# RWKV section of a three-block decoder: low-rank products taken from the unnormalised split, token mixes in two operations through PSUM, key scaling moved ahead

## The reference, cut to what matters

```python
hn = rms_norm(h, g[1])
xx = pad(hn, one token)[:, :-1] - hn              # previous token minus this one
xm = hn[None] + xx[None] * mix[:, None, None, :]  # six token mixes
xr, xw, xk, xv, xa, xg = xm
r, k, v = xr @ w_r, xk @ w_k, xv @ w_v            # 1024 x 1024 each
w_log = -softplus(-(w0 + tanh(xw @ w1) @ w2)) - 0.5   # 1024 -> 64 -> 1024
a = sigmoid(a0 + (xa @ a1) @ a2)                      # 1024 -> 64 -> 1024
g = sigmoid(xg @ g1) @ g2                             # 1024 -> 160 -> 1024
kk = normalised per head (k * k_k);  k = k * (1 + (a - 1) * k_a)
decay = exp(-exp(w_log))
y = scan over tokens(r, decay, k, v, -kk, kk * a);  bonus = sum(r * k * r_k) * v
```

## Time and profile before

| | us |
|---|---|
| median of 3 runs (1629.85 to 1635.62) | 1633.55 |
| the profiled execution, device time | 1638.21 |
| its span on the core | 1636.4 |
| TensorE busy in it | 1573.2 |
| POOL busy | 1132.7 |
| ACT busy | 775.7 |
| DVE busy | 659.9 |

### The profile page before, as it was taken

The page is one execution under the profiler, slowest core; times in us unless marked ns, Lnnn a source line. Parts: engine busy times, 40 slices in busy tenths (PEclk is TensorE's granted clock), DMA queues, the critical chain, the costliest instruction groups (busy, mean ns, idle before and its releaser), DMA issues.

```text
span 1636.4 us, 40796 instructions
## 1 busy us (share of the span) xinstructions
PE 1573.2 (96%) x16206; PEld 1498.9 (92%) x16206; DVE 659.9 (40%) x1534; ACT 775.7 (47%) x1271; POOL 1132.7 (69%) x835
## 2 busy tenths in 40 slices
PE   6999989899999999999999999999999999999998
PEld 6999989688887999999999987599999988799998
DVE  4332067664545433223332257743351434433200
ACT  5444447832314544445444442654445534655532
POOL 6787858683505787788777785068878984468885
PEclk9999999898999999999999999999999998999999
DMA  6453533320012554465544641055545542235552
GB/s 251 178 181 128 182 115 112 129 88 3 3 54 78 181 179 163 142 208 180 179 155 146 213 160 52 2 196 201 183 147 185 193 158 90 94 107 195 187 180 77
DMA packets 37910, 231.34 MB, mean 141 GB/s; under 512 B 4527, under 2 KB 6680, under 8 KB 16552
## 3 DMA queue, kind: packets, MB, share of 16 engines
...
...
## 4 chain that ended last, share of the span: by engine, by line
PE 90%; DVE 5%; issue 2%; POOL 2%; ACT 1%; DMA 1%; SPq 0%; DVEq 0%; POOLq 0%; ACTq 0%
PE PS L768 74%; PE PS L767 2%; POOL wlo L722 1%; PE PS L999 1%; PE PS L1006 1%; PE PS L1014 1%; PE PS L1376 1%; PE PS L1164 1%; PE PS L1155 1%; DMA raw<-w_f_in_in 1%; PE PS L783 0%; PE PS L1038 0%; PE PS L1044 0%; DVE ktmp L1983 0%; PE PS L989 0%
## 5 line engine op out<-in xcount | busy, mean ns | idle before, releaser
L722 POOL TENSOR_TENSOR wlo<-raw,whi 128x256 fp32r<-128x256 f32 (+2 forms) x759 | 1085.9, 1464 | 445.4 <-ACT whi L2524 418.2
L768 PE MATMUL PS<-xh,whi 128*128 128x272 f32 (+1 forms) x2336 | 676.2, 289 | 23.2 <-POOL wlo L722 17.9
L768 PE MATMUL PS<-xl,whi 128*128 128x272 f32 (+1 forms) x2336 | 668.4, 286 | 0.0
L768 PE MATMUL PS<-xh,wlo 128*128 128x272 f32 (+1 forms) x2336 | 667.8, 286 | 0.0
L2524 ACT ACTIVATE whi<-raw 128x1024 fp32r<-128x1024 f32 x472 | 459.7, 982 | 390.1 <-PE PS L768 363.5
L768 PEld LDWEIGHTS PS<-xh,whi 128*128 128x128 f32 x2336 | 440.4, 189 | 31.8 <-issue 24.3
L768 PEld LDWEIGHTS PS<-xh,wlo 128*128 128x128 f32 x2336 | 442.2, 189 | 0.0
L768 PEld LDWEIGHTS PS<-xl,whi 128*128 128x128 f32 x2336 | 441.6, 189 | 0.6
L768 PE MATMUL PS<-hid_h,whi 128*128 128x272 f32 (+1 forms) x960 | 273.6, 285 | 1.6 <-POOL wlo L722 1.6
L768 PE MATMUL PS<-hid_h,wlo 128*128 128x272 f32 (+1 forms) x960 | 273.8, 285 | 0.0
L768 PE MATMUL PS<-hid_l,whi 128*128 128x272 f32 (+1 forms) x960 | 272.8, 284 | 0.0
...
## 6 DMA issues: line engine op xcount, KB each, us to landing
...
```

The source lines that it names most:

```text
L722: last = nc.gpsimd.tensor_tensor(wlo[U % SPL][:, piece], raw[U % RAW][:, piece], whi[U % SPL][:, piece].bitcast(F32), ALU.subtract)
L768: mm(out, a, b, start=start and n == 0, stop=stop and n == 2, **kw)
```

## The change

- Low-rank products: `lora_wa` and `lora_g` leave the list of units. Their weights are loaded once, and during `f0_dn` (one of 8 chunks per output chunk) DVE scales them by mix and by 1 - mix into PSUM, ACT copies the high parts, DVE subtracts the low parts (`lora_weights`). `f0_dn` now also splits `h` times the gain into `xh[0]`, `xl[0]`, and its DVE and ACT loops are written out. TensorE takes the products for decay, a and gate from that split; DVE multiplies both results by `rstd` and adds the one shifted by a token (`lora_drain`).
- The order on TensorE becomes: first products of decay and a, half of the gate's, `wa2` with the gate's other half in three blocks between, `rk_k` (first unit with both output tiles for each input chunk), `rk_r`, `rk_v`. The 64 constant passes go.
- Token mixes: three in place of six. `hn` has a zero column in front, `xx` is gone, and a mix is a `tensor_scalar` of `hn` into PSUM and a `scalar_tensor_tensor` that adds `hn` of the token before. `rstd` is copied to PSUM, from where `hn` is made.
- Head sums move between units 2 and 3 of `rk_r`, `spread_kk` ahead of `rk_v`, `bonus_sums` to the middle of `rk_v`; the key's factor gets a buffer of its own (`Bk`), the keys are scaled in front of `a_g`, and the bonus products wait for `rk_r` by pairs. ACT's copy of `g2` moves behind the bonus copies.

```diff
-    ("rk_k", 4, 4, 2048), ("lora_wa", 1, 1, 1024), ("rk_r", 4, 4, 2048), ("wa2", 1, 8, 1024),
-    ("lora_g", 1, 1, 1280), ("rk_v", 4, 4, 2048),
+    ("wa2", 1, 8, 1024), ("rk_k", 4, 4, 2048), ("rk_r", 4, 4, 2048), ("rk_v", 4, 4, 2048),
...
+                if name == "f0_in" and i is None and u == 5:
+                    sp.dma_start(raw_wa[:, :, :], t["w_lora_wa"][0].rearrange("p (k c) -> p k c", k=KC)).then_inc(s_lraw, 16)
...
+            sp.dma_start(raw_g[:, :, :], t["w_lora_g"][0].rearrange("p (k c) -> p k c", k=KC)).then_inc(s_lraw, 16)
...
+                if paired and u == 0:
...
+                    for k in range(KC):
+                        pe.wait_ge(s_x, X0[x] + k + 1)
+                        for mi in range(2):
+                            c = mi * 1024 + k * 128
+                            last = products(PS[:, bank(G) + mi, 0:n], weights(U, ALLR, slice(c, c + 128)),
+                                            (xh[b][:, k, 0:n], xl[b][:, k, 0:n]), k == 0, k == KC - 1)
+                    last.then_inc(s_unit, 2)
+                    continue
...
+    def lora(w_, which, out, at, m, ks):
+        h_, l_ = w_
+        for k in ks:
+            c = k * h_.shape[2] // KC + at
+            last = products(PS[0:m, out, 0:T], (h_[:, which, c:c + m], l_[:, which, c:c + m]),
+                            (xh[0][:, k, :], xl[0][:, k, :]), k == 0, k == KC - 1)
+        return last
...
+    pe.wait_ge(s_ldr, KC)
+    first_lora(0, range(KC - 1))
     norm_sum("rk", T)
-    constants(44, PS[:, 1, 0:128])
-    project("rk_k", T, 1, "m0", wide=True)
-
-    U, G = U0["lora_wa"], G0["lora_wa"]
-    pe.wait_ge(s_lo, 2 * U + 2)
...
-    pe.wait_ge(s_free, G - 1)
-    constants(20, PS[:, bank(G), 0:128])
-    project("rk_r", T, 3, "m3")
+    first_lora(1, range(KC - 1))
+    first_lora(0, (KC - 1,))
+    first_lora(1, (KC - 1,)).then_inc(s_lora, 1)
+    gate_lora(0, range(KC)).then_inc(s_lora, 1)
...
     for m in range(KC):
+        if m in (2, 4, 6):
+            if m == 2:
+                pe.wait_ge(s_ldr, KC + 3)
+            last = gate_lora(1, {2: range(3), 4: range(3, 6), 6: range(6, 8)}[m])
+            if m == 6:
+                last.then_inc(s_lora, 1)
         G = G0["wa2"] + m
         pe.wait_ge(s_free, G - 1)
         for mi in range(2):
...
             last = products(PS[:, bank(G) + mi, 0:T], weights(U, r, slice(m * 128, m * 128 + 128)),
                             (lh_h[r, :], lh_l[r, :]), True, True)
         last.then_inc(*((s_part, 1) if m < KC - 1 else (s_unit, 2)))
...
+    project("rk_k", T, 1, "m0", paired=True)
...
+    project("rk_r", T, 3, "m1", between={2: kk_sums})
+    project("rk_v", T, 0, "m2", between={0: spread_kk, 2: bonus_sums})
...
+        if beside:
+            for m in range(8):
+                beside(m)
+                add(m, None)
+                after_act(m, None)
+            return
...
-    residual("f0_dn", T, 1, 2, 0.5, "rk", None, None)
+    v.tensor_scalar(unmix[:, :], vec[:, VEC["rk_mix"]:VEC["rk_mix"] + 48], -1.0, 1.0, ALU.mult, ALU.add).then_inc(s_wa, 1)
...
+        for b_, a, z, which in ((4, 0, 64, 1), (4, 64, 128, 4), (6, 0, 160, 5)):
+            src = raw_wa if b_ == 4 else raw_g
+            for mixed_ in range(2):
+                c = 8 * which + k
+                m = col(VEC["rk_mix"] + c) if mixed_ else unmix[:, c:c + 1]
+                last = v.tensor_scalar(PS[:, b_ + mixed_, T + a:T + z], src[:, k, a:z], m, None, ALU.mult)
...
+    def lora_low(k):
+        dve.wait_ge(s_lhi, k + 1)
+        for h_, l_, b_, n in ((wide_wa_h, wide_wa_l, 4, 128), (wide_g_h, wide_g_l, 6, 160)):
+            o = slice(k * n, k * n + n)
+            last = v.tensor_tensor(l_[:, :, o], PS[:, b_:b_ + 2, T:T + n], h_[:, :, o].bitcast(F32), ALU.subtract)
...
+    residual("f0_dn", T, 1, 2, 0.5, "rk", norm_col(0, 1), "rk", beside=lora_weights)
...
+    def lora_drain(out, rows, bank_, n, dst, signal):
+        dve.wait_ge(s_lora, n)
+        step.do(v.tensor_tensor(shifted[out][0:rows, 1:T + 1], PS[0:rows, bank_ + (2 if out == 0 else 1), 0:T],
+                                rstd[0:rows, :], ALU.mult))
+        ps = PS[0:rows, bank_, 0:T]
+        step(v.tensor_tensor(ps, ps, rstd[0:rows, :], ALU.mult))
+        v.tensor_tensor(dst, ps, shifted[out][0:rows, 0:T], ALU.add).then_inc(signal, 1)
+    lora_drain(0, 128, 1, 1, PS[:, 1, 0:T], s_ldr)
...
+    step(v.tensor_copy(PS[:, 7, 0:T], rstd[:, :]))
...
+            step.do(v.scalar_tensor_tensor(hn[:, c, 1:T + 1], h[:, c, :], col(norm_col(0, 1) + c), PS[:, 7, 0:T],
                                            ALU.mult, ALU.mult))
...
-        step.do(v.tensor_tensor(xx[:, q, 1:T], hn[:, q, 0:T - 1], hn[:, q, 1:T], ALU.subtract))
-        step(v.tensor_scalar(xx[:, q, 0:1], hn[:, q, 0:1], -1.0, None, ALU.mult))
...
-            v.scalar_tensor_tensor(mixed_chunk(c), xx[:, c, :], col(VEC["rk_mix"] + 8 * which + c), hn[:, c, :],
-                                   ALU.mult, ALU.add).then_inc(s_xm, 1)
...
+        step.do(v.tensor_scalar(mixed_chunk(s, c), hn[:, c, 1:T + 1], unmix[:, m:m + 1], None, ALU.mult))
...
+        v.scalar_tensor_tensor(mixed_chunk(s, c), hn[:, c, 0:T], col(VEC["rk_mix"] + m), mixed_chunk(s, c),
+                               ALU.mult, ALU.add).then_inc(s_xm, 1)
...
+    normed(0, 2)
+    dve.wait_ge(s_lhi, KC + 1)
+    low(lh_l[:, :], lh[:, :], lh_h[:, :], s_ldr)
+    normed(2, 6)
+    lora_drain(1, 80, 4, 2, gh[:, 0, :], s_ldr)
+    normed(6, 8)
+    step.sync()
+    for c in range(KC + 1):
+        if c < KC:
+            if c >= 2:
+                dve.wait_ge(s_x, X0["m0"] + c - 1)
+            mix_begin(0, c)
+            step.sync()
+            mix_add(0, c)
+        if c:
+            mix_end(0, c - 1)
+    lora_drain(1, 80, 4, 3, gh[:, 1, :], s_ldr)
...
-    for s in (1, 2, 3):
-        mix(s, 0)
-        mix(s, 1)
...
-    low(lh_l[:, :], lh[:, :], lh_h[:, :], s_lhl)
...
-    for s in (4, 5):
-        mix(s, 0)
-        mix(s, 1)
...
+    for s in (1, 2):
...
+                mix_begin(s, c)
+            step.sync()
+            for c in range(4 * half, 4 * half + 4):
+                mix_add(s, c)
+            for c in range(4 * half, 4 * half + 4):
+                mix_end(s, c)
+    dve.wait_ge(s_ghh, 1)
+    low(gh_l[0:80, :, :], gh[:, :, :], gh_h[0:80, :, :], s_ghl)
...
+    def bonus_products(pair):
+        dve.wait_ge(s_free, G0["rk_r"] + pair + 1)
+        for c in (2 * pair, 2 * pair + 1):
+            v.scalar_tensor_tensor(ktmp[:, c, 0:T], R_[:, c, 0:T], col(VEC["r_k"] + c), K_[:, c, 0:T],
+                                   ALU.mult, ALU.mult).then_inc(s_rkr, 1)
+    bonus_products(0)
+    bonus_products(1)
     for c in range(KC):
         dve.wait_ge(s_kkb, c + 1)
         v.tensor_tensor(A_[:, c, 0:T], A_[:, c, 0:T], PS[:, 4 + c % 4, 0:T], ALU.mult).then_inc(s_kkd, 1)
+    dve.wait_ge(s_dk, 1)
+    v.tensor_tensor(a_g[:, :, :], a_g[:, :, :], W_[:, :, 0:T], ALU.mult).then_inc(s_rks, 1)
+    bonus_products(2)
+    bonus_products(3)
+    dve.wait_ge(s_unit, 2 * U0["rk_v"])
...
+                    if k == 0 and steps:
+                        steps(j)
...
+        turns(step, 8 // w, per, 0, body, 8 // w if steps else 1)
...
+        act.wait_ge(s_wa, k + 2)
+        for h_, b_, n in ((wide_wa_h, 4, 128), (wide_g_h, 6, 160)):
+            last = f(h_[:, :, k * n:k * n + n], PS[:, b_:b_ + 2, T:T + n], ACT.Copy)
+        last.then_inc(s_lhi, 1)
+    residual("f0_dn", T, 1, 2, "rk", "rk", steps=lora_high)
...
+    hi(U0["rk_k"])
+    act.wait_ge(s_ldr, KC + 1)
+    step.do(f(lh[0:64, :], PS[0:64, 1, 0:T], ACT.Tanh))
+    step.do(f(lh[64:128, :], PS[64:128, 1, 0:T], ACT.Copy))
...
+    f(lh_h[:, :], lh[:, :], ACT.Copy).then_inc(s_lhi, 1)
+    f(warm[:, :], vec[:, 0:1], ACT.Sigmoid)
...
-        if m == 1:
-            hi(U0["lora_g"])
+        if m >= 1:
+            mixed(0, (m - 1,))
+    hi(U0["rk_k"] + 1, only=(0,))
+    mixed(0, (7,))
+    hi(U0["rk_k"] + 1, only=(1,))
+    act.wait_ge(s_ldr, KC + 4)
+    step(f(gh[:, :, :], gh[:, :, :], ACT.Sigmoid))
+    f(gh_h[0:80, :, :], gh[:, :, :], ACT.Copy).then_inc(s_ghh, 1)
+    hi(U0["rk_k"] + 2)
+    drain("rk_k", 0, K_)
+    mixed(1, range(0, 4))
+    hi(U0["rk_k"] + 3)
+    drain("rk_k", 1, K_)
...
+    drain("rk_k", 3, K_)
+    mixed(2, range(4, 8))
+    for c0 in range(0, KC, 2):
+        direction(c0)
+    act.wait_ge(s_kk, KC)
+    f(ktmp[:, :, 0:T], A_[:, :, 0:T], ACT.Square).then_inc(s_kksq, 1)
+    hi(U0["rk_r"] + 2)
+    drain("rk_r", 0, R_)
...
+        f(Bk[:, c, :], a_g[:, c, :], ACT.Identity, scale=vec[:, VEC["k_a"] + c:VEC["k_a"] + c + 1],
+          bias=lessk[:, c:c + 1]).then_inc(s_kg, 1)
+    hi(U0["rk_r"] + 3)
+    drain("rk_r", 1, R_)
+    act.wait_ge(s_lora, 4)
+    f(knorm[0:16, :], PS[0:16, 4, 0:T], ACT.Sqrt).then_inc(s_kkr, 1)
     hi(U0["rk_v"])
...
-    f(knorm[0:16, :], PS[0:16, 4, 0:T], ACT.Sqrt).then_inc(s_kkr, 1)
     act.wait_ge(s_cum, KC)
```

(6 more changed lines are left out.)

248 lines of the change are left out of this document (102 added, 146 removed).

## The result

The changed kernel takes 1623.51 us (median of 4 runs, 1619.50 to 1625.76), the kernel before 1634.05 in the same session: a ratio of 0.9937 (95% interval 0.9920 to 0.9953), a gain of 10.5 us by the medians. I had forecast 1606.5 us, a gain of 27, and a range of 1600 to 1619. The direction was right, the size was not.

What follows compares the result with a forecast made beforehand. No engine alone bounded 216.3 to 353.3 us: 99 us TensorE work, 38 waits and slow clock. Scan start 353.3 - 324.1 = 29 us, less 2 for hand-offs, gain 27: 1611 us profiled, 1606.5 median; range 1600 to 1619.

Steps and rivals of the forecast that it cites:

- The front: Behind `f0_dn`, TensorE goes straight on from 216.3 us and ends the gate's first half at 228.7.
- rivals 2 and 4: In `f0_dn`: 2, ACT late 1 us a chunk, 1614.5 us, chance 0.08; 4, POOL holds scalings, 1652.5 us, chance 0.04.
- `wa2` and the gate's other half: After the gate's first half, TensorE needs 9.0 us and ACT 8.9; taken as 9.4 us, ending at 238.1.
- first mix: At `rk_k`'s start, TensorE takes mixed chunks from 238.1 us, the last split at 242, and ends unit 0 at 244.1.
- Then 11 units: From unit 0 to TensorE's end: 66 us of units plus head sums, `spread_kk` and bonus sums, ending at 322.2 us.
- 88 x 0.70 + 10: POOL's pieces from `rk_k`'s third unit to `g2`: 72 us with 10 for DVE's products, ending at 320.2 with idle time.
- rival 1: Before the scan, POOL sets the pace: gain 25 at 0.88 us a piece, 1617.5 us at 1.0; chance 0.14.
- 2 us of allowance: In the sum up to the scan, 2 us left for unseen hand-offs, taking the gain from 29 to 27 us.
- Rival 3: At the front and in `wa2`, TensorE waits at half clock without constants: costs 4 us, 1610.5 us; chance 0.08.
- 4.5 us on the path: Before the scan, removing the constants takes 4.5 us off the path; the rest of them lie in the front.

Runs made afterwards that it cites:

- e3: Changed kernel with rk_k's first unit waiting for the last but one drain of wa2 in place of the last; median 1620.9 us, ratio 0.9918.
- e2: Changed kernel with DVE's last row of two-SBUF-input products cut to one column or memsets, so the output is wrong; median 1617.2 us, ratio 0.9890.
- e1: Changed kernel with 14 constant passes on TensorE before rk_v's last unit and 18 before `scaled`; median 1617.8 us, ratio 0.9895.
- f1: Changed kernel with rk_k's first unit waiting for the last but one drain, and POOL pieces of 512 columns, not 256; median 1619.5 us, ratio 0.9897.
- e4: Changed kernel with POOL's low parts of rk_k, rk_r, rk_v and g2 in pieces of 1024 columns, not 256; median 1621.3 us, ratio 0.9913.
- the repetition: Changed kernel run once more as it is, against the kernel before; median 1623.2 us, ratio 0.9936.
- f4: Kernel before without its constant passes (44 before rk_k, 20 before rk_r); median 1639.3 us, ratio 1.0027.

## Why the prediction was wrong

**The front.** TensorE did go on without a gap behind `f0_dn`: 96 passes and the sum from 216.9 to 229.5, 12.6 us for my 12.4. `f0_dn` kept its pace (8.28 us from addition to addition), and the scalings took what the nearest rows had said:

```profile
L1965 DVE TENSOR_SCALAR PS<-lora_wa_raw,unmix x16: 276/284/291, 153.0 to 211.5; 128x64 f32<-128x64 f32 x16
L1965 DVE TENSOR_SCALAR PS<-lora_g_raw,unmix x8: 376/378/383, 153.7 to 211.9; 128x160 f32<-128x160 f32 x8
```

Only its first chunk was longer (9.12 us, 8.20 before), and TensorE's part of the stage ended 0.6 us later than in the profile of the kernel before. So rivals 2 and 4 fell: the six scalings were never held by POOL. For these operations, which write to PSUM, the hold that I had taken from the Trainium skill's "SBUF — State Buffer", section "Who interferes with whom", did not come; that section makes it depend on the operands, which my use of it left out. Then the sum slipped. Step "`wa2` and the gate's other half", 9.4 us, took 10.8 (229.47 to 240.26): a group of `wa2` took 1.0 us, 4.1 in all for the 3.0 that I had, and 0.4 us were a wait. Step "first mix", by which unit 0 runs beside the mixes from 238.1 and ends at 244.1: it started at 241.96, behind ACT's last sigmoid, and ended at 248.3. I had read the mixes as its only condition and passed over the wait at G in the diff. e3 measured 1.05 us for the wait; the last mix ended at 243.84, 1.8 later than predicted, and was covered. Together with `f0_dn`'s later end and the 0.2 us at the front this makes 4.2 us.

**"Then 11 units".** Predicted 78.1 us from unit 0's end to TensorE's; measured 330.28 - 248.3 = 82.0. Waits for POOL are 2.9 of it. The 11 units took 67.6 us in place of 66.5, and the three sums 11.4 in place of 11.6.

**POOL.** The step that failed is "88 x 0.70 + 10": the addition for the products measured 78.7 - 61.6 = 17.1 us. I had argued that half of the 20 us before came from the mixes and would go; with the mixes through PSUM the first 32 pieces did run at 0.70, but the last 56 cost 17 more than that. 10.6 of these are shown to be the products' by e2; the other 6.5 are put down to them because the long pieces among the middle 32 stand beside DVE's running sums, products and the reciprocal. The products are as many as before; before, the a_g product fell in a stretch of 5.5 us where POOL stood idle, and now POOL idles for 0.5 us there. The mean piece was 0.895: rival 1 at its lower price, which I had at 0.14. POOL's own end came at 332.3 us in place of 320.2: it began 4.2 us later, behind unit 0, its pieces took 6.7 us more and its idle time was 1.1 longer. That made TensorE wait (2.9 us) and cost another 1.6 us at `scaled` (3.5 us from TensorE's end to the scan in place of 1.9). Rival 1's price for 1.0 us a piece, 1617.5, had moreover left out the 2 us of allowance that its price for 0.88 has; with it the time would be some 1619.5.

4.2 + 3.9 + 1.6 = 9.7 us: the scan at 333.8 in place of 324.1.

**Behind the scan's start.** My sum ended there and took the rest as unchanged; it is 7.1 us longer in the profiles (1290.2 against 1283.1 to the span's end), and 8 to 9 by the medians. That is the largest single term missed, put at nothing without a reason. Rival 3 had spoken of the clock, but at the front and in `wa2`, where it was whole. The lost time is clock, as far as the runs tell: over all the kernels the scan's length follows its time at half clock, from 145.1 us with 14.5 of it (e1) to 157.3 with 47 (f1), about 0.4 us for each, while DVE, ACT and POOL have the same work. What makes the spells longer is settled in part. Constants ahead of the scan shorten it in the changed kernel: rest 1287 to 1290 with none or 3, 1282 to 1285 with 8 to 16 (11 and 16 no better than 8), 1279 with 32. A gap in the kernel before, 3.4 us larger, cost 0.9 to 2 us beyond itself. So "the new gap put the scan on half clock", which I had taken for the cause, is not enough: e2 and e4 have no gap over 0.2 us at `scaled`, and have the long rest all the same, and the repetition started its scan at full clock and had it too. For e2:

```profile
328.37 0.54 PE L998 MATMUL PS<-ident,scaled 64*96 64x64 f32 x12 [0.18 <-POOL scaled L690]
```

Open stays what in the changed kernel's way to the scan does it.

9.7 + 7.1 = 16.8, less the 2 us of allowance: the 14.8 us between 1611 and 1625.8. The mechanisms of the gain were as predicted (19.5 of 29 us up to the scan are there); the terms for POOL, for unit 0 and for the clock in the scan were not.

The constants "4.5 us on the path" was wrong too, as f4 shows: their removal alone gains nothing. In the changed kernel TensorE has no wait in front of `rk_r`, as the mix is there in time; that took the 4.5 us away.

On POOL the Trainium skill, "SBUF — State Buffer", section "Who interferes with whom", says that a DVE instruction with two SBUF inputs contends with a GpSimd instruction that reads SBUF, and the later one blocks. The trace agrees in both directions: 2.64 us for a product of 0.5 behind a piece of 1024, and 10.6 us lost by 24 pieces.
